# Hymba decoder step on one core: how the first activations, the small vectors and the first table load are asked for

## What is computed

```python
n = rmsnorm(h, norm_mix)
z, xbc, dt, q, k, v = split(n @ w_in)      # 4112 columns
y_ssd = gated_norm(ssd_scan(silu(conv(xbc)), dt), z)
y_att = rmsnorm(dilated_window_attention(q, k, v))
h = h + concat(y_ssd, y_att) @ w_out
h = h + moe(rmsnorm(h, norm_ffn))          # softmax router, top 4 of 32 experts, SwiGLU
y = rmsnorm(h, norm_final)
```

## Time and profile before

| What | us |
|---|---|
| median of three runs (lowest, highest) | 1233.67 (1232.75, 1233.68) |
| the profiled execution's own time | 1234.86 |
| its span, first to last instruction | 1232.7 |
| TensorE busy in it | 1160.5 |
| VectorE busy | 365.5 |
| ScalarE busy | 250.0 |
| DMA, mean over the span | 376 GB/s |

### The profile page before, as it was taken

One profiled execution on the slowest core, in us unless ns is written; L12 is line 12 of the kernel. 1 busy time (PEld: TensorE's weight loads), 2 busy tenths in 40 slices (PEclk: granted clock), 3 DMA queues, 4 the chain that ended last, 5 costly groups with the idle time before them and its releaser, 6 DMA issues.

```text
span 1232.7 us, 14855 instructions
## 1 busy us (share of the span) xinstructions
PE 1160.5 (94%) x5867; PEld 506.8 (41%) x5882; DVE 365.5 (30%) x752; ACT 250.0 (20%) x496; POOL 55.2 (4%) x49
## 2 busy tenths in 40 slices
PE   9999999899999999999989898989898989898997
PEld 6777656534433434333333333333232323232332
DVE  2457335765512132221203030303122121212122
ACT  2014443627320211112011111111111111020113
POOL 0000032621000000000000000000000000000000
PEclk9999999999999999999999999999999999999999
DMA  9677557379799999999999999999999999999995
GB/s 293 207 250 256 205 183 280 135 254 417 326 426 430 426 427 430 427 430 428 427 430 428 426 431 428 427 430 429 429 429 427 429 428 427 430 427 428 429 427 247
DMA packets 64368, 463.58 MB, mean 376 GB/s; under 512 B 7704, under 2 KB 25268, under 8 KB 38380
## 3 DMA queue, kind: packets, MB, share of 16 engines
q1 hardware_dynamic: 62206, 459.02, 90.5%
q10 hardware_dynamic: 1582, 2.22, 0.5%
q0 software_dynamic: 544, 1.84, 0.4%
HBM read 455.82 MB, written 7.24 MB: 376 GB/s over the span
## 4 chain that ended last, share of the span: by engine, by line
PE 57%; DMA 38%; DVE 2%; issue 1%; ACT 1%; SPq 0%; DVEq 0%; ACTq 0%
DMA ring<-in_w 34%; PE ps L2436 21%; PE ps L1909 10%; PE ps L2460 5%; DMA own<-in_w 3%; PE ps L2354 2%; PE ps L2362 2%; PE ps L2323 2%; PE ps L2356 1%; PE ps L2194 1%; PE ps L1951 1%; PE ps L2372 1%; PE ps L2422 1%; PE ps L1985 1%; PE ps L1928 1%
## 5 line engine op out<-in xcount | busy, mean ns | idle before, releaser
L2436 PE MATMUL ps<-ring,own 128*64 128x512 f32 x1456 | 326.5, 595 | 31.4 <-DMA ring<-in_w 31.4
L2436 PEld LDWEIGHTS ps<-ring,own 128*64 128x64 f32 x1456 | 104.1, 137 | 236.0 <-issue 178.3
L1763 DVE TENSOR_SCALAR own<-ps 128x512 f32<-128x512 f32 x32 | 22.1, 692 | 556.8 <-PE ps L2436 556.8
L2436 PE MATMUL ps<-own 128*64 128x512 f32 x592 | 134.1, 594 | 11.8 <-DMA own<-in_w 11.8
L2460 PE MATMUL ps<-ring,own 128*64 128x512 f32 x592 | 133.5, 595 | 5.4 <-issue 5.2
L1909 PE MATMUL ps<-own,ring 128*128 128x288 f32 x512 | 131.4, 412 | 0.0
L1909 PEld LDWEIGHTS ps<-own,ring 128*128 128x128 f32 x512 | 96.1, 192 | 29.2 <-issue 4.5
L2460 PE MATMUL ps<-own 128*64 128x512 f32 x432 | 98.4, 595 | 3.9 <-issue 2.6
L2436 PEld LDWEIGHTS ps<-own 128*64 128x64 f32 x592 | 43.2, 137 | 95.1 <-issue 84.5
L2460 PEld LDWEIGHTS ps<-ring,own 128*64 128x64 f32 x592 | 44.0, 137 | 82.9 <-issue 72.5
L1151 ACT ACTIVATE own<-ps 64x512 f32<-64x512 f32 x60 | 35.5, 592 | 205.6 <-PE ps L2460 204.8
(11 more groups left out here) (384 smaller groups left out, 1003.1 us busy)
## 6 DMA issues: line engine op xcount, KB each, us to landing
ring<-in_w SPq DMA_DIRECT2D x128, 2048.0 KB, 38.6
own<-in_w SPq DMA_DIRECT2D x63, 2048.0 KB, 37.4
ring<-in_w_in SPq DMA_DIRECT2D x16, 1024.0 KB, 7.7
ring<-in_cache_win_k SPq DMA_DIRECT2D x8, 1024.0 KB, 5.8
ring<-in_cache_win_v SPq DMA_DIRECT2D x8, 1024.0 KB, 4.9
ring<-in_w_out SPq DMA_DIRECT2D x6, 1024.0 KB, 10.9
ring<-in_state_ssm SPq DMA_DIRECT2D x8, 512.0 KB, 7.3
out_ssm_sample<-ring SPq DMA_DIRECT2D x8, 512.0 KB, 8.6
```

What stands on the lines that cost most here:

```text
L1763: nc.vector.tensor_scalar(xg_o, hid[:, 0], LIMIT, None, ALU.min).then_inc(sem("glu_ready"), 1)
L2436: last = nc.tensor.matmul(ps[C * half:C * half + C, 1 + m, :], xT[:, k, C * u:C * u + C], rows[:, D * half + 512 * m:D * half + 512 * m + ...
```

## The change

The prompt comes in two transfers, tile 0 first, then the samples, then tile 1; tiles 0 and 2 share the semaphore `x02_in`, tile 1 has `x1_in`. TensorE transposes tile by tile (0, 2, 1), all eight pieces of each, and tells of the pieces as those of the last tile are done; the pieces 6 and 7 are no longer left for later. The eight small vectors are asked for by SyncE, behind item 0 and the constants and ahead of the ring's next item. ScalarE asks for the identity alone before its first square root, and for the convolution rows after the four copies of pieces. ScalarE waits for `x02_in`, VectorE for `x1_in` alone.

```diff
         @block.sync
-            sp.dma_start(h[:, 0:2, :], a["x_prompt"][0].rearrange("(i p) d -> p i d", p=P)).then_inc(sem("x_in"), 16)
-            sp.dma_start(h[0:NS, 2, :], a["x_sample"].rearrange("b t d -> (b t) d")).then_inc(sem("x_in"), 16)
+            sp.dma_start(h[:, 0, :], a["x_prompt"][0, 0:P]).then_inc(sem("x02_in"), 16)
+            sp.dma_start(h[0:NS, 2, :], a["x_sample"].rearrange("b t d -> (b t) d")).then_inc(sem("x02_in"), 16)
+            sp.dma_start(h[:, 1, :], a["x_prompt"][0, P:2 * P]).then_inc(sem("x1_in"), 16)
...
                 if n == 0:
                     sp.dma_start(consts[:, 2 * P:], a["consts"][:, 2 * P:]).then_inc(sem("const_in"), 16)
+                    sp.dma_start(rows_small[0:8, 0:P], a["norm_mix"][0].rearrange("(k p) -> k p", p=P)).then_inc(sem("vec_in"), 16)
...
+                    sp.dma_start(rows_small[0:1, P + 48:P + 80], a["router_b"]).then_inc(sem("vec_in"), 16)
         @block.scalar
             act.dma_start(consts[:, 0:2 * P], a["consts"][:, 0:2 * P]).then_inc(sem("ident_in"), 16)
-            act.dma_start(rows_small[0:8, 0:P], a["norm_mix"][0].rearrange("(k p) -> k p", p=P)).then_inc(sem("vec_in"), 16)
...
-            act.dma_start(rows29[28:29, :], a["conv_b"]).then_inc(sem("rows_in"), 16)
             act.wait_ge(zeroed, 3)
             nc.scalar.activation(stat[:, 61:62], stat[:, 60:61], ACT.Sqrt)
-            act.wait_ge(sem("x_in"), 32)
+            act.wait_ge(sem("x02_in"), 32)
...
                 nc.scalar.activation(xnT[:, k, :], ps[:, k, 0:TOK], ACT.Copy).then_inc(sem("xnT_act"), 1)
+            act.dma_start(rows29[0:24, :], a["state_conv"][0].rearrange("b t c -> (b t) c")).then_inc(sem("rows_in"), 16)
+            act.dma_start(rows29[24:28, :], a["conv_w"][0]).then_inc(sem("rows_in"), 16)
+            act.dma_start(rows29[28:29, :], a["conv_b"]).then_inc(sem("rows_in"), 16)
         @block.vector
-            dve.wait_ge(sem("x_in"), 32)
+            dve.wait_ge(sem("x1_in"), 16)
         @block.tensor
-            pe.wait_ge(sem("x_in"), 32)
-            for k in range(6):
-                first_tokens(k)
+            for c in TILE_ORDER:
+                if c == 1:
+                    pe.wait_ge(sem("x1_in"), 16)
+                else:
+                    pe.wait_ge(sem("x02_in"), 32)
+                for k in range(KT):
+                    last = nc.tensor.transpose(ps[:, k, cols(c)], h[0:ROWS[c], c, k * P:(k + 1) * P], ident[0:ROWS[c], 0:ROWS[c]])
+                    if c == TILE_ORDER[-1]:
+                        last.then_inc(sem("xnT_ps"), 1)
...
-            for k in range(6, KT):
-                first_tokens(k)
```

More of the change, by code:

```diff
@@ L637, in _ @@
                     sp.dma_start(consts[:, 2 * P:], a["consts"][:, 2 * P:]).then_inc(sem("const_in"), 16)
+                    sp.dma_start(rows_small[0:8, 0:P], a["norm_mix"][0].rearrange("(k p) -> k p", p=P)).then_inc(sem("vec_in"), 16)
+                    sp.dma_start(rows_small[8:16, 0:P], a["norm_ffn"][0].rearrange("(k p) -> k p", p=P)).then_inc(sem("vec_in"), 16)
+                    sp.dma_start(rows_small[16:24, 0:P], a["ssd_norm"][0].rearrange("(k p) -> k p", p=P)).then_inc(sem("vec_in"), 16)
+                    sp.dma_start(rows_small[24:28, 0:P], a["att_norm"][0].rearrange("(k p) -> k p", p=P)).then_inc(sem("vec_in"), 16)
+                    for i, name in enumerate(("dt_bias", "a_log", "d_skip")):
+                        sp.dma_start(rows_small[0:1, P + 16 * i:P + 16 * i + 16], a[name]).then_inc(sem("vec_in"), 16)
+                    sp.dma_start(rows_small[0:1, P + 48:P + 80], a["router_b"]).then_inc(sem("vec_in"), 16)
             w1 = a["w1"][0].rearrange("e (s p o) c -> e s p (o c)", p=P, o=W1_ROWS)
@@ L1815, in stay_busy @@
                 nc.tensor.matmul(ps[:, bank, 0:n], ident, consts[:, 0:n], start=True, stop=True)
[L1818 to L1822, removed]
             pe.wait_ge(zeroed, 2)
```

## The result

The changed kernel takes 1236.31 us (median of 18 runs, 1234.63 to 1239.14) where the kernel before takes 1233.58 in its 18 runs beside them: the ratio is 1.0023, 95% interval 1.0017 to 1.0030. It is slower by 2.7 us. One run of a later version (e3) took 2406 us, belongs to a slow state and stands in no ratio. The profiled execution of the changed kernel took 1236.01 us with a span of 1233.9.

What follows compares the result with a forecast made beforehand. It took TensorE's chain in the opening as the bound, moving the rest one to one. Projection 0's start +0.8 and clock -0.2 gave +0.6 us: 1233.67 + 0.6 = 1234.3 us, no measurable difference; range 1232.2 to 1236.4.

Steps and rivals of the forecast that it cites:

- the third rival: Opening: vectors land at 13.2 us, first matmul +2.1, longer half-speed stretch +1.3; +3.4 us, 1237.1; chance 0.12.
- The bound, and one to one: Whole kernel: a microsecond won or lost in the opening moves all the rest about one to one.
- Three transfers: Activations' arrival: tiles 0 and 2 land at 5.5 us, tile 1 between 6.35 and 7.06, no later than before.
- TensorE tile by tile: Opening transposes: start at 6.35 instead of 7.20; 24 at 0.18 us take 4.3, delaying the reciprocals' transposes 0.25 us.
- ScalarE's table first: ScalarE's opening: table loaded by about 3 us, square root at 8.5 instead of 9.31; reciprocals 0.8 us sooner, worth nothing.
- The vectors on SyncE: Small vectors behind w_in and constants on SyncE's queue: land at 11.9 us, so TensorE waits 0.75 us; the deciding term.
- the upper bound: Vectors' latest landing: behind the constants plus eight small packets and their semaphores, 12.74 + 0.5 = 13.2 us.
- The convolution rows later: ScalarE's late convolution rows: land by about 18 us, read at 21.94; cost zero, with 4 us of cover.
- From the vectors to projection 0: Vectors' transpose to first matmul: multiplication at 12.83, first matmul at 13.4 instead of 12.57 us, 0.8 us late.
- The clock: Projection 0: half-speed stretch stays, ending at 15.45 us or moving with the work; taken as 0.2 us less.
- Against what: Baseline: +0.6 us charged against the profiled execution's 1234.86, its half-speed stretch included, then put on the runs' median, 1233.67.

Runs made afterwards that it cites:

- e3: Changed kernel with the eight vectors still on SyncE's queue, but right behind tile 1 and ahead of w_in; ratio 0.9997 to the kernel before.
- e8: Kernel before with only the convolution rows asked for later, after the copies; ratio 0.9990 to the kernel before.
- e1: Changed kernel with the eight vectors back on ScalarE's queue; ratio 1.0002 to the kernel before, median 1233.73 us.
- e2: Kernel before with only the eight vectors moved to SyncE's queue behind the constants; ratio 1.0050 to the kernel before.
- e7: Kernel before with vectors moved to SyncE and convolution rows asked for after the copies, no transfers by tile; ratio 1.0010, median 1236.31 us.
- e4: Changed kernel with eight matmuls on zeros in TensorE's three gaps of the opening; ratio 1.0010 to the kernel before.

## Why the prediction was wrong

It held the time at the edge of its range (1236.31 of 1236.4), and by luck: it forecast +0.6 us and no measurable difference, where the runs show 2.7 us, with an interval from 2.1 to 3.7. Two terms of its sum failed, by about as much each: the start of projection 0, taken as +0.8 us and measured as +1.70, and the clock, taken as -0.2 and measured as +0.84. The course was that of the third rival, the slower one, to which it gave 0.12, though not with that rival's numbers. Step by step:

- *The bound, and one to one.* Right by the medians: the opening's loss is +2.54 us in the pair of traces and +2.73 in the medians. That the two lie so near is partly luck, since the opening of before that was traced was itself slow; against e8's 16.66 the changed one is 4.05 us late. The pair's spans would have said +1.2, for the later half-clock stretch that only one of them has.
- *Three transfers.* Tiles 0 and 2 were taken to land at 5.5 and landed at 5.42 (1.22 + 4.2). Tile 1 came at about 7.4 (1.68 + 5.7), 0.3 later than the bound. In the changed kernel the wait for the vectors covers that; in e1, where this wait is gone, tile 1's landing heads the chain.
- *TensorE tile by tile.* The start was right (6.20 against 6.35). The cost was wrong: 24 transposes took 2.67 us, 0.11 each, not 4.3 us at 0.18. The 0.18 came from a row in which shapes alternate, 128, 128 and 32 rows; in tile order equal shapes follow each other, and each transpose writes another piece of `ps` than the one before. Which of the two makes the difference, no run tells apart. The faster transposes were no gain: TensorE was done at 8.87 instead of 10.7 and stood idle until 9.91, since the reciprocals were the bound: the work that I had counted as cover for them wasn't there.
- *ScalarE's table first.* Loaded at 2.50, and worth nothing, as forecast, but for another reason: the square root at 8.84 waits for VectorE's sum of tile 1, and the vectors come later than the reciprocals.
- *The vectors on SyncE.* The mechanism was right, and the sum short by 0.48 us: their transpose started at 12.38, not 11.9. The constants landed at 11.9, where 12.74 less 0.8 had put them; but I let the vectors land with them, and kept the eight packets' 0.5 us for the upper bound. They landed at 12.33. The Trainium skill's page "DMA: Bandwidth & Descriptors", section "Issuing engines are not separate DMA queues", says that asking on several engines at once saves only the time of issue. That rule alone doesn't give what happened: against e3, the changed kernel asked for the last vector 1.5 us later and its packets ended 4.3 us later, behind 2.5 MB. The same page's section "Queues, rings and completion order" has each DMA engine take a ring's descriptors in order, and the traces agree: behind w_in and the constants the vectors were 1.5 us late (12.38 against 10.89), on the other queue or ahead of w_in they were no wait (e1, e3).
- *The convolution rows later.* Right that it costs nothing (e8), and it left out what the move is there for: with the vectors gone from ahead of them, an early request of the rows would have cost far more (e2 against e7).
- *From the vectors to projection 0.* This is the first term that failed: the first matmul started at 14.27, not 13.4. Of the 0.87 us, 0.48 are the vectors' landing. Another 0.29 lie between the vectors' transpose and VectorE's first multiplication, 1.22 us instead of the 0.93 of before; the transposes there ran at half clock (0.30 us instead of 0.22, and 0.69 instead of 0.42 for the one-row matmuls behind them), which the sum left at nothing. The last 0.1 is the hand-over from VectorE.
- *The clock.* This is the second. I wrote that "a half-speed stretch" is kept, that it would end at 15.45 or move with the work, and took 0.2 us less. It ended at 18.90: 4.63 us of projection 0 at half clock against 2.88. The 1.75 us more at half speed make the +0.84 inside projection 0 (about half of 1.75). The prediction had the clock stay low no longer than before and gave TensorE's idle time no price of its own; the third rival had one, 1.3 us, under the condition that held (vectors after 12.2), but worked out for vectors at 13.2. e4 shows the idle time's part: with zeros in the gaps the clock stays at 1.00 in the opening and 2.3 us of it come back, of which the run times keep about half.
- *Against what.* I charged the change against one execution's half-speed stretches. The traced execution of before has two, one in the opening and one at 206.6 us. Of the seven traces without added zeros six have one in the opening (e8 has none); of the four with zeros none has, but each of these four has one between 204 and 236 us, in work that all versions share. What decides where it falls, no run here shows.

## What to carry to other kernels

A small transfer is as late as what stands ahead of it in its queue: before moving one off a busy engine's sequencer, add up the bytes in front of it at its new place, and look at what it stood ahead of at its old one. A wait on TensorE near the start of its dense work has two prices, the wait and the matmuls behind it at half clock; here the two were of like size, and a few matmuls on zeros in the gaps took most of the second back. When a step is worth a microsecond in a thousand, read the clock of the stretch first in both traces: one execution's half-speed stretch, 1.5 to 1.7 us here, is over half as large as the effect.

## What the runs showed that was not expected

- The same opening, to 0.1 us the same starts, was done at 18.17 us with the clock at 0.50 for part of projection 0 and at 16.66 with 1.00 (before and e8). Over 81 runs of before the time goes with the mean granted clock, 1232.3 us at 1.000 and 1237.0 at 0.995.
- Transposes in tile order take 0.11 us each, in piece order with alternating shapes 0.18 (after, before).
- Three transfers of 174 KB together on ScalarE's queue, early, moved the landing of 1.2 MB of activations on the other queue from 7.06 to 8.87 us (e2); asked for late, they left it at 7.14 (e7).
- Zeros held the clock as work does: ten instructions on zeros in a 2.03 us gap, granted clock 1.00 there and in projection 0, where with empty gaps projection 0 ran at 0.50 for 4.63 us (e4, after).
